# A two-block transformer kernel: order of projections and scores in block one

## The reference, cut to what matters

```python
proj = h @ w_in
u_pool = proj[..., :POOL_WIDTH]                       # unit 0, 256 columns
qkv = proj[..., POOL_WIDTH:].reshape(B, S, 3, ATTN_HEADS, HEAD_DIM)
q = partial_rope(qkv[:, :, 0], cos, sin) * (HEAD_DIM ** -0.5)
k = partial_rope(qkv[:, :, 1], cos, sin)
v = qkv[:, :, 2]
for g, (window, dilation) in enumerate(((128, 1), (512, 4), (2048, 16))):
    o, l = dilated_window_attention(q[group g], k[group g], v[group g], window, dilation)
alpha = softmax(lse over the three groups)
attn = sum(alpha * o over the three groups)           # 512 x 256
pool = causal_multiscale_pool(u_pool, w_pool, b_pool, pool_scale)
return concatenate([pool, attn]) @ w_out
```

## Time and profile before

| what | value |
|---|---|
| median of 3 executions | 1664.28 us (1662.15 to 1668.35) |
| profiled execution: its time | 1666.63 us |
| profiled execution: span from first to last instruction | 1664.8 us |
| mean granted clock of TensorE | 0.967 |
| TensorE busy with matmuls | 1555.7 us, 93% of the span |
| VectorE / ScalarE / GpSimd busy | 588.2 / 664.9 / 713.9 us |

### The profile page before, as it was taken

The page is one execution under the profiler, slowest core; times in us unless marked ns, Lnnn a source line. Parts: engine busy times, 40 slices in busy tenths (PEclk is TensorE's granted clock), DMA queues, the critical chain, the costliest instruction groups (busy, mean ns, idle before and its releaser), DMA issues.

```text
span 1664.8 us, 19895 instructions
## 1 busy us (share of the span) xinstructions
PE 1555.7 (93%) x7670; PEld 1260.4 (76%) x7670; DVE 588.2 (35%) x928; ACT 664.9 (40%) x987; POOL 713.9 (43%) x608
## 2 busy tenths in 40 slices
PE   7899978899999999999989889999899999999996
PEld 4699757688888888788855568787687788887885
DVE  3665442523333100422034430342325555555001
ACT  2442453444444322322344443453333555544231
POOL 0467103535545544545411136335524554455442
PEclk8999987999999999999999999999999999999999
DMA  8463015322232223234210123122311222322221
GB/s 368 159 271 141 27 68 110 82 98 82 94 101 88 85 86 95 76 102 135 84 45 30 38 102 115 51 76 80 132 55 51 86 90 101 101 81 83 90 86 65
DMA packets 28491, 162.73 MB, mean 98 GB/s; under 512 B 4584, under 2 KB 4840, under 8 KB 13704
## 3 DMA queue, kind: packets, MB, share of 16 engines
q1 hardware_dynamic: 24960, 151.05, 26.4%
q10 hardware_dynamic: 3464, 10.74, 2.5%
HBM read 157.04 MB, written 4.74 MB: 97 GB/s over the span
## 4 chain that ended last, share of the span: by engine, by line
PE 70%; issue 10%; POOL 8%; DVE 6%; DMA 3%; ACT 2%; POOLq 0%; SPq 0%; ACTq 0%; DVEq 0%
PE ps L1693 60%; POOL WL L774 7%; DMA adaw<-w_ada_dram 2%; PE ps L1659 1%; PE ps L1902 1%; DMA raw<-w_up_dram 1%; PE ps L1916 1%; PE ps L1929 1%; DVE S L1584 1%; POOL WL L738 1%; DVE ps L1299 1%; DVE S L1571 1%; PE ps L1826 1%; DVE xT L1304 1%; DVE md L1574 0%
## 5 line engine op out<-in xcount | busy, mean ns | idle before, releaser
L738 POOL TENSOR_TENSOR WL<-raw,WH 128x512 fp32r<-128x512 f32 (+2 forms) x344 | 369.7, 1103 | 584.2 <-ACT WH L854 584.1
L1693 PE MATMUL ps<-hH,WH 128*128 128x512 f32 x1136 | 461.1, 406 | 22.2 <-POOL hL L752 9.3
L1693 PE MATMUL ps<-hL,WH 128*128 128x512 f32 x1136 | 453.9, 400 | 0.0
L1693 PE MATMUL ps<-hH,WL 128*128 128x512 f32 x1136 | 453.4, 399 | 0.0
L774 POOL TENSOR_TENSOR WL<-raw,WH 128x512 fp32r<-128x512 f32 x176 | 246.3, 1430 | 253.9 <-ACT WH L1014 253.9
L1693 PEld LDWEIGHTS ps<-hH,WH 128*128 128x128 f32 x1136 | 216.8, 191 | 79.5 <-issue 25.3
L1693 PEld LDWEIGHTS ps<-hH,WL 128*128 128x128 f32 x1136 | 216.6, 191 | 53.2
L1693 PEld LDWEIGHTS ps<-hL,WH 128*128 128x128 f32 x1136 | 216.8, 191 | 50.4
L854 ACT ACTIVATE WH<-raw 128x1024 fp32r<-128x1024 f32 (+3 forms) x172 | 148.1, 885 | 234.8 <-PE ps L1693 231.2
L1693 PE MATMUL ps<-hidH,WH 128*128 128x512 f32 x352 | 137.9, 392 | 1.1 <-POOL WL L774 1.1
L1693 PE MATMUL ps<-hidL,WH 128*128 128x512 f32 x352 | 137.0, 389 | 0.0
(11 more groups left out here) (275 smaller groups left out, 2221.9 us busy)
## 6 DMA issues: line engine op xcount, KB each, us to landing
raw<-w_up_dram SPq DMA_DIRECT2D x44, 1024.0 KB, 4.9
raw<-w_in_dram SPq DMA_DIRECT2D x36, 1024.0 KB, 4.9
adaw<-w_ada_dram SPq DMA_DIRECT2D x20, 1024.0 KB, 7.1
raw<-w_down_dram SPq DMA_DIRECT2D x16, 768.0 KB, 4.2
raw<-w_down_dram SPq DMA_DIRECT2D x16, 640.0 KB, 3.9
adap<-w_ada_dram SPq DMA_DIRECT2D x4, 1024.0 KB, 18.1
xT<-x_dram ACTq DMA_DIRECT2D x2, 2048.0 KB, 10.2
raw<-w_mem_kv_dram SPq DMA_DIRECT2D x4, 1024.0 KB, 4.7
```

The costliest lines, as they stand in the source:

```text
L738: pool.tensor_tensor(WL[:, d % 2, ks, cols], raw[:, d % 2, ks, cols], WH[:, d % 2, ks, cols].bitcast(F32), ALU.subtract).then_inc(lo_done, 1)
L1693: mm = pe.matmul(out, lhs[x], rhs[y], start=(first and i == 0), stop=(last and i == 2))
```

## The change

The order of units becomes queries and keys of group 0, values of group 0, queries and keys of group 1, queries and keys of group 2, values of group 1, values of group 2. The weights are packed in this order on the host. The six turns move with their units, to steps 2, 3, 5, 6, 7 and 8 (they were at 2, 3, 5, 6, 8 and 9).

The score tiles are put beside units 4 to 9 by a table `FRONTS`: its key `(d, 0)` is the place between the two halves of unit `d`, `(d, 1)` the place behind its second half, evacuation and split. Tiles 0 to 5 all use banks 6 and 7, which the turns use too, so a turn waits until the tile before it is read (`TILE_BEFORE_TURN`) and a tile until the turn before it is read. The score storage is moved: tiles 0, 1, 3 and 4 lie where the low part of `h` was, tile 2 in another free place, and `PT1` moves.

A TensorE step `seed` behind `pool` clears the two output banks of the sums (which stood in `back(0)` before) and has ten and eight small matmuls on `ones` into bank 7. The pool's evacuation is cut into six steps that stand behind blocks 1, 3, 5, 7, 9 and 11. `WHOLE_EXP` has tile 6 in place of tile 5.

```diff
-WHOLE_EXP = (5, 7, 9, 11)
-SCORE_BANKS = [((4, 5), (6, 7))[i] for i in (0, 1, 0, 0, 1, 0, 1, 0, 1, 0, 1, 0)]
+WHOLE_EXP = (6, 7, 9, 11)
+SCORE_BANKS = [((4, 5), (6, 7))[i] for i in (1, 1, 1, 1, 1, 1, 0, 0, 1, 0, 1, 0)]
+QKV = ((0, 0), (0, 1), (0, 2), (1, 0), (1, 1), (2, 0), (2, 1), (1, 2), (2, 2))
+FRONTS = {(4, 0): (0,), (4, 1): (1,), (5, 0): (2,), (6, 0): (3,), (7, 0): (4,), (8, 0): (5, 6), (8, 1): (7,),
+          (9, 0): (8, 9), (9, 1): (10, 11)}
+TURNS_READ = {0: 4, 3: 6, 4: 8, 5: 10, 8: 12}
+TILE_BEFORE_TURN = {2: 2, 3: 3, 4: 4, 5: 5}
...
+def turned_at(d):
+    return 2 <= d < D_OUT and QKV[d - 2][1] < 2
...
             if d == ADA_REST:
                 steps += [("ada_end", 2)]
-            if d >= ADA_REST:
-                steps += [("front", 3 * (d - ADA_REST)), ("front", 3 * (d - ADA_REST) + 1)]
+            steps += [("front", n) for n in FRONTS.get((d, 0), ())]
...
-            if d == ADA_REST:
-                steps += [("front", 2)]
+            steps += [("front", n) for n in FRONTS.get((d, 1), ())]
...
-        steps += [("front", 5), ("pool",)] + [("front", n) for n in range(6, len(TILES1))] + [("weights",), ("split", D_OUT + 1)]
-        steps += [("scale", n) for n in SUM_ORDER] + [("mid", 0)]
+        steps += [("pool",), ("seed",), ("weights",), ("split", D_OUT + 1)] + [("scale", n) for n in SUM_ORDER] + [("mid", 0)]
+        pool_at = {1: ("pool_out", 0, 0), 3: ("pool_out", 0, 1), 5: ("pool_hi", 0), 7: ("pool_out", 1, 0), 9: ("pool_out", 1, 1), 11: ("pool_hi", 1)}
...
-            if i in (3, 7):
-                steps += [("pool_out", i // 4)]
+            if i in pool_at:
+                steps += [pool_at[i]]
...
+            def seed():
+                scores_read(pe, len(TILES1) - 2)
+                for _ in range(10):
+                    pe.matmul(ps[:, 7, 0:P], ones[:], ones[:], start=True, stop=True)
+                scores_read(pe, len(TILES1) - 1)
+                for q in range(2):
+                    pe.matmul(ps[:, 4 + q, :], ident_r[:], mask[:, P:P + 1].broadcast_to([P, S]), start=True, stop=False)
+                for _ in range(8):
+                    pe.matmul(ps[:, 7, 0:P], ones[:], ones[:], start=True, stop=True)
...
-                if i == 0:
-                    for q in range(2):
-                        pe.matmul(ps[:, 4 + q, :], ident_r[:], mask[:, P:P + 1].broadcast_to([P, S]), start=True, stop=False)
...
-    given["w_in"] = packed(inputs["w_in"], [0] + [UC + part * 768 + g * UC for g in range(GROUPS) for part in range(3)])
+    given["w_in"] = packed(inputs["w_in"], [0] + [UC + part * 768 + g * UC for g, part in QKV])
```

More of the change, by code:

```diff
@@ L113, with qkv_unit @@
 NEAR = TT
-WHOLE_EXP = (5, 7, 9, 11)
-SCORE_BANKS = [((4, 5), (6, 7))[i] for i in (0, 1, 0, 0, 1, 0, 1, 0, 1, 0, 1, 0)]
+WHOLE_EXP = (6, 7, 9, 11)
[5 more added lines that the diff above has]
+TILE_BEFORE_TURN = {2: 2, 3: 3, 4: 4, 5: 5}
+def qkv_unit(g, part):
+    return 1 + QKV.index((g, part))
+def turned_at(d):
+    return 2 <= d < D_OUT and QKV[d - 2][1] < 2
 SUM_ORDER = list(range(NEAR, len(TILES1))) + list(range(NEAR))
@@ L220, in build @@
         V1 = at("V1", [P, TT, GROUPS, UC], 57)
-        S1 = at("S1", [P, 14, S], 69)
-        S1z = at("S1z", [P, 1, S], 17)
-        PT1 = at("PT1", [P, 4, S], 0)
+        S1 = at("S1", [P, 7, S], 69)
+        S1n = nc.alloc_sbuf_tensor_at("S1n", [P, KD, S], F32, offset=front + 2 * tile_bytes)
+        S1m = at("S1m", [P, 2, S], 0)
+        PT1 = at("PT1", [P, 4, S], 83)
         cosT = at("cosT", [P, GROUPS, TT, 8], 98)
@@ L449, in build @@
             steps += [("seg", d, 0, 4 if d == D_IN else 0, KD)]
-            if d >= 2 and (d - 1) % 3 in (1, 2):
+            if turned_at(d):
                 steps += [("rope", r)]
@@ L619, in scores @@
         def scores(n):
-            nk, i = TILES1[n][2], key_blocks(n)
-            t = S1z[:] if n == len(TILES1) - 1 else S1[:, i:i + nk, :]
+            t = (S1n[:, 4:5, :], S1n[:, 5:7, :], S1m[:], S1n[:, 2:4, :], S1n[:, 7:8, :])[n] if n <= NEAR else S1[:, n - 5:n - 4, :]
             return t.rearrange("p k c -> p (k c)").rearrange("p (x w) -> p x w", x=GH)
@@ L941, in evac_in @@
                 else:
-                    g, part = (d - 1) // 3, (d - 1) % 3
+                    g, part = QKV[d - 1]
                     src = banks(d).rearrange("p b (t n) -> p (b t) n", t=2)
@@ L964, in masks, with pool_out, pool_hi @@
                 sc.activation(ident_r[:], ident, ACT.Copy).then_inc(masks_ready, 1)
-            def pool_out(m):
+            def pool_out(m, half):
                 sc.wait_ge(pool_done, m + 1)
-                if m == 0:
+                if m == 0 and half == 0:
                     sc.dma_start(xT[:], a["x"]).then_inc(x_back, 16)
[L970 to L974, removed]
+                r = slice(64 * half, 64 * half + 64)
+                sc.activation(win[r, m, 0:S], ps[r, 2 * m + half, :], ACT.Identity,
+                              bias=small[r, 16 + m:17 + m], scale=v("pool_scale", m)[r, :]).then_inc(pool_val, 1)
+            def pool_hi(m):
                 sc.wait_ge(pool_val, 2 * m + 2)
@@ L980, in front @@
                 if n == 0:
+                    for count, tiles in zip(spread_lo, (4, 2, 2)):
+                        sc.wait_ge(count, tiles)
+                elif n == NEAR + 1:
                     sc.wait_ge(ada_turned, len(ADA_DVE))
@@ L1147, in _ @@
                   "spread_hi": spread_hi_tile, "spread_lo": spread_lo_tiles, "evac_in": evac_in, "turn": turn,
-                  "masks": masks, "pool_out": pool_out, "front": front, "weights": weights, "mid": mid, "attn_out": attn_out, "evac_y": evac_y, "up": up,
+                  "masks": masks, "pool_out": pool_out, "pool_hi": pool_hi, "front": front, "weights": weights, "mid": mid, "attn_out": attn_out, "evac_y": evac_y, "up": up,
                   "bias_fetch": bias_fetch, "bias_rows": bias_rows, "evac_in2": evac_in2, "bias_load": bias_load, "evac_br": evac_br,
@@ L1384, in turn @@
                 g, part = e // 2, e % 2
-                d = 1 + 3 * g + part
+                d = qkv_unit(g, part)
                 ve.wait_ge(banks_read[pair_of(d)], bank_use(d) + 1)
@@ L1601, in _ @@
                   "finish": finish, "evac_in": evac_in,
-                  "spread_lo": spread_lo_tiles, "rope": turn, "pool_out": pool_out, "front": front, "weights": weights, "scale": scale,
+                  "spread_lo": spread_lo_tiles, "rope": turn, "pool_hi": pool_hi, "front": front, "weights": weights, "scale": scale,
                   "attn_out": attn_out, "up": up,
@@ L1788, in turn @@
                 pe.wait_ge(rope_done, 2 * e + 2)
-                if e >= 4:
-                    scores_read(pe, (1, 4)[e - 4])
+                if e in TILE_BEFORE_TURN:
+                    scores_read(pe, TILE_BEFORE_TURN[e])
                 for hp in range(2):
@@ L1810, in front @@
                 g, b, nk = TILES1[n]
-                pe.wait_ge(turn_read, 12 if n >= 6 else 10 if n == 4 else 4 * g + 4)
+                if n in TURNS_READ:
+                    pe.wait_ge(turn_read, TURNS_READ[n])
                 if n == 0:
                     pe.wait_ge(masks_ready, 2)
+                if n == 6:
                     pe.wait_ge(mod_ready, 3)
@@ L1843, in back @@
                 last = i == len(SUM_BLOCKS) - 1
-                if i == 0:
-                    for q in range(2):
-                        pe.matmul(ps[:, 4 + q, :], ident_r[:], mask[:, P:P + 1].broadcast_to([P, S]), start=True, stop=False)
-                pe.wait_ge(banks_read[pair_of(3 + 3 * g)], bank_use(3 + 3 * g) + 1)
+                pe.wait_ge(banks_read[pair_of(qkv_unit(g, 2))], bank_use(qkv_unit(g, 2)) + 1)
                 pe.wait_ge(pt_read, i + 1)
@@ L1932, in _ @@
             walk({"ada_row": ada_row, "row_turn": row_turn, "ada_turn": ada_turn, "warm": warm, "squares": squares, "norm": norm, "sums": sums, "cross_sums": cross_sums,
-                  "spread_y": lambda n: spread(n, 0), "spread_x": lambda n: spread(n, 1), "twin": twin, "seg": seg, "turn": turn, "pool": pool_step, "front": front,
+                  "spread_y": lambda n: spread(n, 0), "spread_x": lambda n: spread(n, 1), "twin": twin, "seg": seg, "turn": turn, "pool": pool_step, "seed": seed, "front": front,
                   "mid": mid, "back": back, "up": up, "bias_rows": bias_rows, "front2": front2,
```

## The result

The changed kernel takes 1657.73 us (median of 7, 1655.89 to 1661.45), the kernel before 1666.11 us in the runs beside it (median of 7); ratio 0.995, 95% interval 0.9934 to 0.9966. That is 8.4 us faster, where 9.6 were forecast. Its profiled execution took 1657.42 us (before 1666.63), its span is 1655.6 us and its mean granted clock 0.970. The difference came out near the forecast; the time itself lies at the upper end of the forecast's 1652 to 1658, as the kernel before came out 1.8 us higher too. One term of the sum was wrong by 4.3 us, and smaller errors and what changed outside the stage hid part of that.

A forecast was written before the change was run, and what follows sets the result against it. Bound: TensorE, 70% of the chain, and a ping-pong behind unit 9. Terms -12.2 + 5.3 + 0.3 - 1.85 + 0.9 - 2.3 = -9.85, rounded to 9.6; 1664.3 - 9.6 = 1654.7 us, range 1652 to 1658.

The forecast's parts named there:

- The tail: From unit 9's end to the first transpose of the sums: 9.0 us in place of 21.2, minus 12.2 us.
- Tiles and turn in the units: On TensorE: five score tiles plus 5.4, last turn plus 0.9, wait for modulation columns minus 1.0; plus 5.3 us.
- The cover of unit 5: Turn waiting for tile 2 on banks 6 and 7: 13.7 us against TensorE's 13.6; stall 0 to 1, taken 0.3.
- Rival A: Units 5 to 7: shared banks make turns wait, clock may fall; 3 to 4 us, about 1658.3 us; chance 0.16.
- wrong if turns wait for tiles: Trace sign against the forecast; units 4 to 9 were to show no TensorE wait for exponentials over 0.5 us.
- Units 6 and 7: Their turns start without a maximum ahead of the rotation, so have 1.5 us and more to spare.
- The start of the sums: First transpose to end of first `back`: 2.3 us for 4.15, minus 1.85; clock loss from the gap, plus 0.9.
- The pool: Evacuation in six steps removes `back`'s waits for ScalarE's copy, minus 2.5 us; 0.2 comes back, so minus 2.3.
- The exchange through DRAM: SyncE's queue, behind the load of unit 12: cost 0, up to 2 us if that load holds it up.
- Rival B: Load at 253.34 behind the output projection is held by something that doesn't move: end stays at 1664; chance 0.05.
- Rival C: Clock falls before the sums, stays low through key blocks (rule: transposes don't count for full clock): 1668.8 us; chance 0.05.
- D: Unit order or steps do not take effect as drawn, tiles 6 to 11 behind unit 9 again: 1660; chance 0.08.

The follow-up runs named there:

- tiles 8 to 11 behind: Changed kernel with score tiles 8 and 9 moved from between unit 9's halves to behind unit 9, with 10 and 11: 1659.31 us, ratio 0.9969 to before.
- rotation first: Changed kernel with the rotation of unit 4's queries moved ahead of tile 1 on VectorE: 1653.37 us, ratio 0.9927 to the kernel before.
- split behind the rotation: Changed kernel with GpSimd's low part of unit 6 waiting until unit 4's rotation is done: 1658.35 us, ratio 0.9953 to the kernel before.
- pool in two: Changed kernel with the pool's evacuation put back into two places, behind blocks 3 and 7: 1658.64 us, ratio 0.9958 to the kernel before.

## Why the prediction was right, and where not

- **The tail, forecast 9.0 us in place of 21.2, minus 12.2.** Right: 8.5 us, minus 12.7. The run with tiles 8 to 11 behind shows that the place of the tiles sets the tail: with two of them moved back it grew by 6.6 us.
- **Tiles and turn in the units, plus 5.3.** Right in what the parts cost: a tile of 1.08 us (181.23 and 181.66), no wait for the modulation columns. Measured, unit 9's copy-out is 9.9 us later than before; 4.6 of this is the next point.
- **The cover of unit 5, "equal to a tenth", 0.3 us taken.** This step failed. The sum used the rotation's 2.45 us from a place where five of its six instructions ran ahead of GpSimd. I had put it behind tile 1's maximum (measured, it starts 3.3 us later within the stage) and did not look at what would then run beside it. The bound given for this stall, 0 to 1 us, was too narrow: it measured 3.05 us, and the clock behind it cost 1.5 (7.19 against 5.65), which I had as a rival's price and not in the term. That is 4.6 against 0.3. Rival A described this outcome, a turn that waits and a slow half unit behind it, at 0.16. The shared banks that it named are why the turn waits for tile 2's exponentials, but not why these came late; its 1658.3 lies nearer to the measured 1657.73 than the forecast's 1654.7. The prediction's own sign, "wrong if turns wait for tiles", came true, and unit 9's end at 203.51, the first transpose at 212.03 and the last `back` at 230.35 all lie behind the stretches that it gave for them. The run with the rotation first and the one with the split behind it show the cause from two sides.
- **Units 6 and 7 "have 1.5 us and more to spare".** No turn waited there in the changed kernel, nor in the runs with the rotation first. But the spare was counted with a rotation at its own speed: with the split's wait alone the rotation of unit 5 took 6.4 us, and the turn of that rotation waited 2.62 us.
- **The start of the sums, minus 1.85 plus 0.9.** The first `back` ends 2.4 us behind the first transpose, as worked out; the loss of 0.9 did not come, since TensorE had no gap there. I had sized the small matmuls by the mask's columns at 1.9 us for all; ten took 2.3 and eight 1.9, so they filled the gap of 2.3 us that I had left. The trace lists the ten as x20 and the eight as x16, two records for each of these fp32 products, where the mask's, whose operands are marked fp32r, has one. The run without them shows what the gap costs when it is there: 0.86 us, near the 0.9 I had taken.
- **The pool, minus 2.3.** Right: the wait fell from 2.5 us to 0.2, and putting it back cost 2.44.
- **The exchange through DRAM, 0.** Right: no wait for it in the trace.
- **Rival B** is refuted: the load keeps its 21.47 us and moves with the stage. **Rival C and its rule** (the Trainium skill, TensorE: Matmul & The Clock Gate, Part 4: PE-mode transpose) did not come, nor did D, as all steps stand where they were drawn: the blocks, half of them transposes, ran at 1.00 for 17 us, and in the run without small matmuls the clock rose again inside the blocks.
- **The sum.** In the trace, the stage up to the load is 7.4 us shorter, where -9.85 was summed: 4.3 less by the cover, against 0.5 more by the tail and 1.2 more in the blocks, with 0.15 more behind them. The rest of the 9.2 us between the two profiled executions lies in the start (0.6) and behind the load (1.2), where nothing was changed and where single executions differ by up to 6 us. The interval of the ratio allows 5.7 to 11.0 us, so that the 8.4 of the medians lies nearer to 9.6 than the stage's 7.4 is chance.

The rule that I should have weighed is in the Trainium skill (GPSIMD Engine Reference, 1. Specifications): GpSimd shares its interfaces to SBUF with VectorE, with contention for instructions of VectorE that have two inputs in SBUF or run in a mode with two ports. The trace agrees for the first kind: three such products went from 0.28 to 1.38 us, and the reduction from PSUM did not change. Whether the small product, slow with one input in SBUF, is of the second kind, no run shows. How much it costs is read from the trace. The sign was there before the change: the rotation that began at 124.20 had five short instructions, and its sixth, which met the start of GpSimd's low part, took 1.39 us:

```profile
125.35 1.39 DVE L1398 TENSOR_TENSOR qtok<-rope 128x128 f32<-128x128 f32 x1
125.19 5.19 POOL L738 TENSOR_TENSOR WL<-raw,WH 128x512 fp32r<-128x512 f32 x4 [7.07 <-ACT WH L854]
```

## What to carry to other kernels

When a step is moved by two microseconds, look up what will run beside it at its new time, on the engine that shares its memory port most of all; its duration from the old place is only a lower bound. A cover of less than one such slowdown is no cover, and it is priced with the clock's loss behind the stall. And when a wait is removed, look at the next unit for the same collision before counting the gain.

## What the runs showed of the hardware

- Beside GpSimd's subtractions of two 128x512 tiles, a VectorE product of two 128x128 tiles in SBUF took 1.38 us in place of 0.28. That is about as long as one of the subtractions (four in 5.28 us, and in 5.03 where no such product ran). A product of 128x4 in SBUF took 0.55 to 1.27 us in place of 0.17 beside these and other instructions of GpSimd. The multiply-adds with their running sum in PSUM (6 in 4.71 us) and the reduction from PSUM (1.22 us) kept their time.
- Behind an idle stretch of 1.9 us ahead of the projection its first 24 matmuls were slow in the kernel before (7.39 us), the changed kernel (7.23), with the split behind the rotation (7.39) and with the pool in two (7.40), and not with the rotation first alone, without small matmuls or with tiles 8 to 11 behind (5.85 us). The length of the gap alone does not decide; what does stays open.
- The clock rose from 1.2 to 2.4 GHz inside the key blocks, with half of the work transposes: without small matmuls it read 0.50 from 212 to 215 and 0.94 from 215 to 218.
